# Wide products for all of u, a bank per tile, with the halves added between the steps of a top-k search

## The reference, cut to what matters

```
q   = (x @ w_q)                                   # 8 heads, 2 halves of 128
sc  = q . subkeys                                 # 128 scores per head and half
s1, i1 = top_k(sc[first half], 16);  s2, i2 = top_k(sc[second half], 16)
cand = s1[:, None] + s2[None, :]                  # 256 candidates per head
top, pos = top_k(cand, 16);  idx = (i1, i2) looked up at pos;  gate = softmax(top)
act  = gelu(u[idx] . x)                           # u: 16384 x 1024
out  = sum over the picks of gate * act * v[idx]  # v: 16384 x 1024
```

## Time and profile before

| | us |
|---|---|
| median of 3 runs (range) | 2779.95 (2778.19 to 2782.13) |
| the profiled execution, its own time | 2781.96 |
| its span in the trace | 2779.7 |
| TensorE busy | 2686.3 (97%) |
| VectorE busy | 1950.4 (70%) |
| ScalarE busy | 1419.6 (51%) |
| GpSimd busy | 708.1 (25%) |

### The profile page before, as it was taken

The page is one execution under the profiler, slowest core; times in us unless marked ns, Lnnn a source line. Parts: engine busy times, 40 slices in busy tenths (PEclk is TensorE's granted clock), DMA queues, the critical chain, the costliest instruction groups (busy, mean ns, idle before and its releaser), DMA issues.

```text
span 2779.7 us, 40328 instructions
## 1 busy us (share of the span) xinstructions
PE 2686.3 (97%) x15488; PEld 2346.3 (84%) x15488; DVE 1950.4 (70%) x3048; ACT 1419.6 (51%) x2352; POOL 708.1 (25%) x314
## 2 busy tenths in 40 slices
PE   8998999999999998879999999999989999999998
PEld 7887999999888886669999998888868888888887
DVE  5656898787666666767987776666677657656784
ACT  4343456666554543534466665555544465343543
POOL 0000898666000000005996662000000020000000
PEclk9999999999999999989999999999999999999999
DMA  5554555444666564335554445666645554113554
GB/s 207 167 189 159 169 181 168 143 145 144 203 192 196 192 195 139 106 133 164 182 181 141 143 144 189 191 195 193 193 145 189 190 164 135 54 54 102 171 190 159
DMA packets 124270, 451.40 MB, mean 162 GB/s; under 512 B 13856, under 2 KB 13984, under 8 KB 123952
## 3 DMA queue, kind: packets, MB, share of 16 engines
q1 hardware_dynamic: 122256, 441.57, 49.3%
q0 software_dynamic: 1824, 7.25, 0.8%
HBM read 446.67 MB, written 2.10 MB: 161 GB/s over the span
## 4 chain that ended last, share of the span: by engine, by line
PE 90%; DVE 5%; POOL 3%; ACT 1%; issue 1%; DMA 0%; DVEq 0%; SPq 0%; POOLq 0%; ACTq 0%
PE ps L468 17%; PE ps L499 11%; PE ps L500 11%; PE ps L501 11%; PE ps L469 8%; PE ps L450 4%; PE ps L452 4%; PE ps L451 4%; PE ps L604 4%; PE ps L486 3%; PE ps L488 3%; PE ps L487 3%; POOL ring_r L2278 2%; PE ps L733 2%; DVE W L1476 2%; DVE x L1476 1%
## 5 line engine op out<-in xcount | busy, mean ns | idle before, releaser
L1026 ACT ACTIVATE hi<-ring 128x1024 fp32r<-128x1024 f32 x830 | 866.5, 1049 | 257.3 <-PE ps L501 92.6
L2278 POOL TENSOR_TENSOR ring_r<-ring,hi 128x1024 fp32r<-128x1024 f32 x260 | 660.2, 2551 | 1261.2 <-ACT hi L1026 1259.7
L1506 DVE TENSOR_TENSOR ring_r<-ring,hi 128x1024 fp32r<-128x1024 f32 x570 | 693.4, 1223 | 273.9 <-ACT hi L1026 273.5
L468 PE MATMUL ps<-xT_r,hi 128*128 128x512 f32 x2016 | 724.4, 402 | 0.6
L469 PE MATMUL ps<-xT_r,ring_r 128*128 128x256 f32 x2016 | 564.3, 280 | 0.0
L468 PEld LDWEIGHTS ps<-xT_r,hi 128*128 128x128 f32 x2016 | 379.7, 188 | 86.2 <-DVE xT_r L1476 2.4
L499 PE MATMUL ps<-hi,oht_r 128*128 128x512 f32 x1040 | 405.2, 390 | 1.8 <-DVE ring_r L1506 1.2
L501 PE MATMUL ps<-hi,oht_r 128*128 128x512 f32 x1040 | 404.8, 389 | 0.0
L500 PE MATMUL ps<-ring_r,oht_r 128*128 128x512 f32 x1040 | 404.8, 389 | 0.0
L469 PEld LDWEIGHTS ps<-xT_r,ring_r 128*128 128x128 f32 x2016 | 381.2, 189 | 0.0
L450 PE MATMUL ps<-xT_r,hi 128*128 128x256 f32 x1232 | 352.8, 286 | 4.3 <-DVE ring_r L1506 2.9
(11 more groups left out here) (233 smaller groups left out, 3464.2 us busy)
## 6 DMA issues: line engine op xcount, KB each, us to landing
ring<-in_peer_u SPq DMA_DIRECT2D x256, 512.0 KB, 3.4
ring<-in_peer_v SPq DMA_DIRECT2D x256, 512.0 KB, 4.3
ring<-in_f SPq DMA_DIRECT2D x132, 512.0 KB, 3.4
ring<-in_ret_vg SPq DMA_DIRECT2D x32, 512.0 KB, 3.4
ring<-in_peer_q SPq DMA_DIRECT2D x32, 512.0 KB, 3.4
ring<-in_ret_qk SPq DMA_DIRECT2D x16, 512.0 KB, 3.4
ring<-in_ret_out SPq DMA_DIRECT2D x16, 512.0 KB, 3.5
ring<-in_in_shift SPq DMA_DIRECT2D x14, 512.0 KB, 3.5
```

The lines of the kernel that those rows point to most:

```text
L468: pe.matmul(b, h, xT[:, k, :], start=k == 0, stop=k == 7, skip_group_check=True)
L1026: hid.done(a.activation(hi[m % NH][:, :], ring[j % NR][:, :], ACT.Copy), j)
L1506: lo_v.done(v.tensor_tensor(low_part[j % NR][:, :], ring[j % NR][:, :], as32(hi[m % NH][:, :]), ALU.subtract), j)
L2278: lo_p.done(p.tensor_tensor(low_part[j % NR][:, :], ring[j % NR][:, :], as32(hi[m % NH][:, :]), ALU.subtract), j)
```

## The change

- Tiles 0 to 61 are computed as tiles 62 to 127 are: by `mat_w`, one bank per tile, two parts of 256 columns in it.
- For each of them ScalarE copies the second part to one of four SBUF buffers (`low_half`), VectorE adds it to the first part and writes the sum to SBUF (`joined`, which releases the bank), and ScalarE takes the gelu of two joined tiles in place.
- `joined` is placed within VectorE's search by a sum of costs written by hand: after each step of the search, tile j is joined once the sum is above `JOIN_LEAD + TILE_US * j`, 14 + 2.78 j.
- In the search one operand of each large elementwise step, and the outputs of several small ones, move to unused columns of bank 7. Three small copies per group are added or retargeted for this.
- In the second half of the u stage there are four `u_sum` buffers instead of two.

`PICK_TILE`, `EXP_TILE`, the set `B7` and the place of `picked(0)` stay as they are.

```diff
+TILE_US = 2.78
+JOIN_LEAD = 14.0
-        u_sum = [sb(f"usum{i}", 256)[:, :] for i in range(2)]
+        u_sum = [sb(f"usum{i}", 256)[:, :] for i in range(4)]
...
-                    if i < GATE_TILE:
-                        mat_t([TILE["peer_u", l * 128 + i + j] for j in range(2)], None, "peer_u", l, i, among=B7)
-                        continue
                     for j in range(i, i + 2):
                         mat_w(TILE["peer_u", l * 128 + j], None, "peer_u", l, j, among=B7)
-                        if j - GATE_TILE < 64:
+                        if 0 <= j - GATE_TILE < 64:
...
                     if i < GATE_TILE:
-                        a.wait_ge(*at(mm, "peer_u", l, i))
-                        act.done(a.activation(W[:, i * 256:i * 256 + 512], ps("peer_u", l, i), ACT.Gelu_apprx_tanh), "gelu", l, i)
-                        empties(act, "peer_u", l, i)
+                        w = W[:, i * 256:i * 256 + 512]
+                        a.wait_ge(*at(dve, "joined", l, i + 1))
+                        act.done(a.activation(w, w, ACT.Gelu_apprx_tanh), "gelu", l, i)
                         return
...
+                def low_half(i):
+                    if i >= 4:
+                        a.wait_ge(*at(dve, "joined", l, i - 4))
+                    a.wait_ge(*at(mm, "peer_u", l, i))
+                    act.done(a.activation(u_sum[i % 4], ps("peer_u", l, i)[:, 256:512], ACT.Copy), "low_half", l, i)
...
                     split(TILE["peer_u", l * 128 + i] + 2)
+                    if 2 <= i < GATE_TILE + 2:
+                        low_half(i - 2)
+                    if i % 2 == 0 and 6 <= i <= GATE_TILE:
+                        gelu(i - 6)
                     if i == GATE_TILE:
                         scaled_hots(0)
                         scaled_hots(1)
-                    if i <= GATE_TILE:
-                        if i % 2 == 0 and i:
-                            gelu(i - 2)
-                    else:
+                    if i == GATE_TILE + 1:
+                        gelu(GATE_TILE - 4)
+                        gelu(GATE_TILE - 2)
+                    if i > GATE_TILE:
...
             def topk(l):
+                spent, joined_tiles = [0.0], [0]
+                def joined(i):
+                    v.wait_ge(*at(act, "low_half", l, i))
+                    step(v.tensor_tensor, W[:, i * 256:i * 256 + 256], ps("peer_u", l, i)[:, 0:256], u_sum[i % 4], ALU.add,
+                         name=("joined", l, i))
+                    empties(dve, "peer_u", l, i)
+                def join_until(n):
+                    while joined_tiles[0] < n:
+                        joined(joined_tiles[0])
+                        joined_tiles[0] += 1
+                def op(us, fn, *args, name=()):
+                    step(fn, *args, name=name)
+                    spent[0] += us
+                    while joined_tiles[0] < GATE_TILE and spent[0] > JOIN_LEAD + TILE_US * joined_tiles[0]:
+                        join_until(joined_tiles[0] + 1)
+                        spent[0] += 0.45
...
+                io = ps("peer_iota", l)
+                sixteen, index, second = io[:, 0:16], io[:, 128:384], io[:, 384:512]
...
-                        step(v.max, P_s16[:, o:o + 8], s[:, c, :])
-                        step(v.max_index, P_i16u[:, o:o + 8], P_s16[:, o:o + 8], s[:, c, :])
+                        op(0.32, v.max, P_s16[:, o:o + 8], s[:, c, :])
+                        op(0.41, v.max_index, P_i16u[:, o:o + 8], P_s16[:, o:o + 8], s[:, c, :])
...
-                    step(v.tensor_copy, P_i16f, P_i16u, name=("sixteen", l, tt))
+                    op(0.5, v.tensor_copy, index, P_i16u, name=("sixteen", l, tt))
                     if tt:
                         picked(0)
...
-                    tt_(cd, b3(sv[:, :, 0, :], [128, 8, 16, 16], 3), b3(sv[:, :, 1, :], [128, 8, 16, 16], 2), ALU.add)
+                    op(0.3, v.tensor_copy, s2, sv[:, :, 1, :])
+                    op(2.3, v.tensor_tensor, cd, b3(sv[:, :, 0, :], [128, 8, 16, 16], 3), b3(s2, [128, 8, 16, 16], 2), ALU.add)
...
-                        tt_(eq, b3(P_jf[z], [128, 128, 16], 2), b3(iota[:, 0:16], [128, 128, 16], 1), ALU.is_equal)
-                        tt_(eh, eh, b3(iv[:, :, z, :], [128, 8, 16, 16], 2), ALU.mult)
-                        red_(P_picks[tt][z], eq, ALU.add)
+                        op(2.3, v.tensor_tensor, eq, b3(P_jf[z], [128, 128, 16], 2), b3(sixteen, [128, 128, 16], 1), ALU.is_equal)
+                        op(2.3, v.tensor_tensor, eh, eh, b3(iv[:, :, z, :], [128, 8, 16, 16], 2), ALU.mult)
+                        op(2.4, v.tensor_reduce, P_picks[tt][z], eq, AX, ALU.add)
...
+                join_until(PICK_TILE[1] - 2)
                 picked(1)
+                return join_until
...
                 one_hots(0)
                 one_hots(1)
+                join_until(GATE_TILE)
                 step(v.memset, W[:, P_ONES[-1][1] * 256:], 1.0)
```

More of the change, by code:

```diff
@@ L1093, in gelu @@
                     if i < GATE_TILE:
-                        a.wait_ge(*at(mm, "peer_u", l, i))
-                        act.done(a.activation(W[:, i * 256:i * 256 + 512], ps("peer_u", l, i), ACT.Gelu_apprx_tanh), "gelu", l, i)
-                        empties(act, "peer_u", l, i)
+                        w = W[:, i * 256:i * 256 + 512]
+                        a.wait_ge(*at(dve, "joined", l, i + 1))
+                        act.done(a.activation(w, w, ACT.Gelu_apprx_tanh), "gelu", l, i)
                         return
                     a.wait_ge(*at(dve, "summed", l, i))
-                    act.done(a.activation(ps("peer_u", l, i)[:, 0:256], u_sum[i % 2], ACT.Gelu_apprx_tanh), "gelu", l, i)
+                    act.done(a.activation(ps("peer_u", l, i)[:, 0:256], u_sum[i % 4], ACT.Gelu_apprx_tanh), "gelu", l, i)
+                def low_half(i):
[3 more added lines that the diff above has]
+                    act.done(a.activation(u_sum[i % 4], ps("peer_u", l, i)[:, 256:512], ACT.Copy), "low_half", l, i)
                 def scaled_hots(g):
@@ L1636, in picked @@
                     b = ps("peer_pick", l, tt)
-                    step(v.tensor_copy, sv3[:, :, tt * 128:tt * 128 + 128], b[:, 0:384].rearrange("p (z t) -> p z t", z=3),
-                         name=("picked", l, tt))
+                    op(0.6, v.tensor_copy, sv3[:, :, tt * 128:tt * 128 + 128], b[:, 0:384].rearrange("p (z t) -> p z t", z=3),
+                       name=("picked", l, tt))
                     empties(dve, "peer_pick", l, tt)
+                io = ps("peer_iota", l)
+                sixteen, index, second = io[:, 0:16], io[:, 128:384], io[:, 384:512]
+                v.wait_ge(*at(mm, "peer_iota", l))
                 for tt in range(2):
@@ L1647, in topk @@
                             v.wait_ge(*at(act, "peer_s", l, tt, c // 4))
-                        step(v.max, P_s16[:, o:o + 8], s[:, c, :])
-                        step(v.max_index, P_i16u[:, o:o + 8], P_s16[:, o:o + 8], s[:, c, :])
-                        step(v.match_replace, sw[:, c, :], P_s16[:, o:o + 8], s[:, c, :], -3e38)
-                        step(v.max, P_s16[:, o + 8:o + 16], sw[:, c, :])
-                        step(v.max_index, P_i16u[:, o + 8:o + 16], P_s16[:, o + 8:o + 16], sw[:, c, :])
-                    step(v.tensor_copy, P_i16f, P_i16u, name=("sixteen", l, tt))
+                        op(0.32, v.max, P_s16[:, o:o + 8], s[:, c, :])
+                        op(0.41, v.max_index, P_i16u[:, o:o + 8], P_s16[:, o:o + 8], s[:, c, :])
+                        op(0.40, v.match_replace, sw[:, c, :], P_s16[:, o:o + 8], s[:, c, :], -3e38)
+                        op(0.32, v.max, P_s16[:, o + 8:o + 16], sw[:, c, :])
+                        op(0.41, v.max_index, P_i16u[:, o + 8:o + 16], P_s16[:, o + 8:o + 16], sw[:, c, :])
+                    op(0.5, v.tensor_copy, index, P_i16u, name=("sixteen", l, tt))
                     if tt:
@@ L1662, in topk @@
                         o = h * 16
[L1663 to L1667, removed]
+                        op(0.46, v.max, P_topv[:, o:o + 8], ch)
@@ L1668, in topk @@
+                        op(0.55, v.max_index, P_posu[:, o:o + 8], P_topv[:, o:o + 8], ch)
+                        op(0.53, v.match_replace, P_cw, P_topv[:, o:o + 8], ch, -3e38)
+                        op(0.46, v.max, P_topv[:, o + 8:o + 16], P_cw)
+                        op(0.55, v.max_index, P_posu[:, o + 8:o + 16], P_topv[:, o + 8:o + 16], P_cw)
                     tv = P_topv.rearrange("p (h k) -> p h k", h=8)
                     e3 = P_ev.rearrange("p (h k) -> p h k", h=8)
-                    tt_(e3, tv, tv[:, :, 0:1].broadcast_to([128, 8, 16]), ALU.subtract, name=("gate_in", l, tt))
+                    op(0.2, v.tensor_copy, second[:, 0:8], tv[:, :, 0])
@@ L1676, in topk @@
-                        step(v.tensor_copy, P_jf[z], P_ju)
+                            op(0.4, v.tensor_scalar, j, P_posu, 15, None, ALU.bitwise_and)
+                        op(0.3, v.tensor_copy, P_jf[z], j)
```

(17 more changed lines are left out.)

9 lines of the change are left out of this document (5 added, 4 removed).

## The result

The changed kernel took 2807.86 us (median of 4 runs, 2806.58 to 2808.30). The kernel before took 2781.04 us on the same chips, ratio 1.0096, 95% interval 1.0083 to 1.0108. It is 26.8 us slower. The forecast was 23.6 slower, 2803.6, in a range of 2794 to 2820.

The account below looks back on a forecast made before the run. TensorE was taken to bound the u stage, with VectorE nearly full beside it. Per layer +11.3 us up to the first gate (wide products' 3.35 saving included) and +0.5 at the gates, twice +11.8, gave 2803.6 us, range 2794 to 2820.

Parts of the forecast that it names:

- The bank of the first picks: u stage, tile 38: TensorE arrives at 388.0, the first picks' bank is released at 400.4, a wait of 12.4 us.
- VectorE's stretch up to the copy: Layer 0, from search start to the end of `picked(0)`: 115.1 us before, 118.0 forecast with shorter steps and 38 joins.
- the join: VectorE's search: 38 joins ahead of `picked(0)` at 0.45 us each, +17.1 us.
- The clock: Behind the wait at tile 38: TensorE runs 5.2 us at half clock and loses 2.6 us.
- Waits ahead of tile 38: u stage: smaller waits for late joins or splits vanish in the wait at tile 38, whose end VectorE's time sets.
- The wide products: TensorE's tiles as wide products: 0.054 us less per tile, 3.35 us per layer over 62 tiles.
- Up to the first gate: Start of tile 62, just ahead of the first gate: from 459.98 to 471.3, +11.3 us a layer.
- The gate stage: Start of the gate stage: VectorE's memset and gate work lose their slack, +0.5 us a layer, bounds 0 and 1.5.
- The rival that VectorE keeps waiting for GpSimd: VectorE's search: a PSUM operand does not free steps; 2820 or 2833 us, 21 to 27 us wait at tile 38; 13%.
- if it is 20 us, the steps did not get shorter: TensorE's idle time at tile 38: a length of 20 us would mean the search's steps had not shortened.
- The rival behind tile 38 (ScalarE's order): Tiles behind 38: ScalarE's `low_half` and `gelu` wait for joins and delay splits, +6 us a layer, 2816 us; 8%.
- The faster rival: No wait at tile 38, as `picked(0)` ends before 388.0 or its bank is wanted later: -5.7 us, 2774; 7%.

Follow-up runs that it names:

- Three different edits: Changed kernel with picks of group 0 ahead of tile 40 (ratio 0.9995 to before) or tile 36 (1.0021), or still ahead of tile 32 but copied earlier (1.0001).
- tile 40: Changed kernel with the picks of group 0 transposed ahead of tile 40 instead of 32: 2779.66 us, ratio 0.9995 to the kernel before.

## Why the prediction was right

It was right in its cause and its direction, and 3 us short in size (26.8 measured, 23.6 forecast). That it came so near is in part luck: a join cost more than forecast, and the pace behind the first picks gave some of it back.

- **The bank of the first picks** was the deciding step. Forecast: TensorE comes to tile 38 at 388.0, the bank is free at 400.4, 12.4 us. Measured 388.4 and 402.6, 14.2 us. Three different edits that separate the release from the request took it away, and one of them left a rest of the size that its shift gives (2.9 us).
- **VectorE's stretch up to the copy** was forecast at 118.0 us and took 402.55 - 281.92 = 120.6. The term that was mis-sized is the join: 0.52 us from start to start, not 0.45, which makes 38 x 0.07 = 2.7 us. The steps themselves came as forecast: large ones 2.29, shift and cast 0.29 each. So did 38 joins ahead of the copy. Without the joins' 38 x 0.52 = 19.8 us the stretch is 100.8, and 100.9 was forecast.
- **The clock**: forecast 2.6 us lost at half clock. The row shows 5.2 us at 0.54. Tile 38 took 5.06 us (402.61 to 407.67) where the tiles behind it took 2.77, so some 2.3 us were lost.
- **Waits ahead of tile 38** do vanish in the long one, as was said. TensorE waited 1.57 us for a late join at 357.0, and the end of the long wait was still set by VectorE's copy:

```profile
357.04 0.48 PE L470 MATMUL ps<-xT_r,hi 128*128 128x512 f32 x1 [1.57 <-DVE W L1486]
```

- **The wide products**: forecast 0.054 us a tile. Up to tile 32 it was that; in tiles 32 to 59 the pace was 0.3467 a step, 0.107 us a tile, by the luck of the pace; in the last two it was 0.3533 again. Together 34 x 0.054 + 28 x 0.107 = 4.8 us instead of 3.35. The trace of before held the faster pace already, in its last feed-forward, and the prediction took only the query's. So 3.35 us a layer were not all that the products can give.
- **Up to the first gate**: the waits 14.2 + 1.6, the clock 2.3, less 4.8 for the wide products and 0.7 for low parts that no longer come late, make 12.6, and 12.5 is what the chain's rows show; +11.3 was forecast.
- **The gate stage** was forecast at +0.5, with 1.5 as its bound. TensorE waited 1.52 us for gate 2, and the rows give 1.8. It was at the bound or a little over it, in both layers. The mechanism was right: moving the memset took the wait away.
- **The rival that VectorE keeps waiting for GpSimd** did not come true: one operand in PSUM frees the step (2.29 against 3.8 to 4.3 with both in SBUF, in the same place). The section "Why PSUM operands drop a tier" of the Trainium skill's "VectorE: DVE Perf Modes" says that a PSUM operand rules out the mode that takes both SBUF ports. The rows fit it: of the small steps that write or read PSUM none waited (0.29 us). Which mode a step ran in, no run shows. The rival's price failed, and with it the sign "if it is 20 us, the steps did not get shorter". With the steps long again the wait at tile 38 stayed at 14.2, and the loss came ahead of it, as waits for low parts. The rival behind tile 38 (ScalarE's order) didn't show: TensorE waited for nothing from 402.7 to the first gate. With both operands in SBUF, though, ScalarE's order did hold up splits.
- **The faster rival** ended near no change and not at 2774. With the wait gone (tile 40) the ratio is 0.9995. In layer 0 that kernel gains 2.3 us up to the first gate (460.28 - 272.21 = 188.07, before 190.34), as two late joins take 2.1 us of the gain, and loses 1.8 behind it, 1.5 of it as the wait for gate 2.

## What to carry to other kernels

When an allocation holds half as much as before, count again who asks for each buffer next. Here a transpose's bank that six pairs of tiles had covered was covered by six tiles, and a copy that was never late became 14 us late, though its place in VectorE's program is the same and it ended only some 5 us later. Price a step put into a full engine from start to start, not by its own duration: 0.52 and not 0.42 us, times 38. An operand in PSUM is worth much where another engine works on SBUF all the time: without it the wide products gained nothing even with no joins (ratio 1.0009), and with it they gained 0.5% (0.9952).

## What the runs showed of the hardware

- The same program runs the same wide products at 0.3467 or 0.3533 us a step in different executions, at the granted clock 1.00. Nothing in these runs says what decides it.
- VectorE and GpSimd slow each other when VectorE reads two operands in SBUF: 3.8 to 4.4 us instead of 2.29, and 2.66 to 2.9 instead of 2.41. With one operand in PSUM neither was slowed. A VectorE step with both in SBUF that started while GpSimd stood idle took 2.29.
- Behind waits of almost the same length TensorE's granted clock stayed at 1.00 in one place (2.88 us) and was 0.59 for 2.6 us in another (2.85 us), in one execution.
